# Differential attention: weights left unscaled by the first map's sum, and the norm by heads merged with the output product

## The reference

```
def mix(p):                                # p: softmax of both maps of a head
    p = p.reshape(b, h2 // 2, 2, nq, nk)
    return p[:, :, 0] - lam * p[:, :, 1]
o = attend(q, k, v, mix)
o = rms_norm(o, subln) * (1.0 - lam_init)  # over the 128 columns of each head, EPS = 1e-6
return o.reshape(B, S, DA_HEADS * DA_V_DIM) @ wo
```

## Time and profile before

| | |
|---|---|
| median of 3 runs | 4159.78 us (4154.15 to 4170.31) |
| the profiled execution | 4156.24 us, span 4154.4 us |
| TensorE, VectorE, ScalarE busy | 92%, 78%, 42% of the span |
| mean granted TensorE clock | 0.970 |

### The profile page before, as it was taken

One profiled execution on the slowest core, in us unless ns is written; L12 is line 12 of the kernel. 1 busy time (PEld: TensorE's weight loads), 2 busy tenths in 40 slices (PEclk: granted clock), 3 DMA queues, 4 the chain that ended last, 5 costly groups with the idle time before them and its releaser, 6 DMA issues. The chain is left out here.

```text
span 4154.4 us, 55430 instructions
## 1 busy us (share of the span) xinstructions
PE 3825.5 (92%) x20565; PEld 3167.5 (76%) x20565; DVE 3236.9 (78%) x6703; ACT 1729.2 (42%) x2866; POOL 986.3 (24%) x788
## 2 busy tenths in 40 slices
PE   4999988987999999999979898888679999999998
PEld 1554678856899999999944656887579999999997
DVE  2563845986999999999932434369979999999997
ACT  1112622256444444444423445322754444444443
POOL 0000000046333333333300000000653333333332
PEclk8999989999999999999989999999899999999999
DMA  4420012069999999999930000120599999999996
GB/s 183 154 98 31 1 61 81 24 211 269 420 415 410 407 405 403 402 406 406 378 117 25 18 35 7 61 81 21 142 336 421 418 405 405 401 405 406 407 405 271
DMA packets 267693, 1033.68 MB, mean 249 GB/s; under 512 B 147009, under 2 KB 150017, under 8 KB 159361
## 3 DMA queue, kind: packets, MB, share of 16 engines
q0 software_dynamic: 76032, 553.68, 33.2%
q1 hardware_dynamic: 191392, 476.46, 30.2%
HBM read 970.69 MB, written 59.39 MB: 248 GB/s over the span
## 5 line engine op out<-in xcount | busy, mean ns | idle before, releaser
L1472 POOL DMA_INDIRECT gbuf<-in_uv,rows x340 | 518.1, 1524 | 877.4 <-DVE hT L1639 807.6
L1264 POOL TENSOR_SCALAR pqT<-iota,selT 128x128 f32<-128x128 f32 x256 | 201.7, 805 | 1514.9 <-ACT selT L1205 1464.7
L1639 DVE SCALAR_TENSOR_TENSOR hT<-gbuf,act,hT 128x1024 f32<-128x1024 f32 x336 | 416.8, 1282 | 6.0
L1624 DVE SCALAR_TENSOR_TENSOR gbuf<-gbuf,ht 128x1024 f32<-128x1024 f32 x340 | 402.0, 1219 | 6.1 <-DMA gbuf<-in_uv,rows 5.9
L1472 POOL DMA_INDIRECT xT<-in_uv,rows x172 | 257.6, 1498 | 469.0 <-DVE hT L1639 394.3
L1486 PE MATMUL ps<-h0h,U0h 128*128 128x384 f32 x1024 | 344.7, 337 | 11.1 <-DVE U0l L1598 11.1
L1486 PE MATMUL ps<-h1h,U1h 128*128 128x384 f32 x1024 | 344.8, 337 | 10.0 <-DVE U1l L1598 10.0
L1486 PE MATMUL ps<-h1h,U1l 128*128 128x384 f32 x1024 | 344.4, 336 | 0.0
L1486 PE MATMUL ps<-h0h,U0l 128*128 128x384 f32 x1024 | 344.3, 336 | 0.0
L1486 PE MATMUL ps<-h1l,U1h 128*128 128x384 f32 x1024 | 344.0, 336 | 0.0
L1486 PE MATMUL ps<-h0l,U0h 128*128 128x384 f32 x1024 | 344.0, 336 | 0.0
(11 more groups left out here) (356 smaller groups left out, 9017.4 us busy)
## 6 DMA issues: line engine op xcount, KB each, us to landing
ring<-in_u SPq DMA_DIRECT2D x128, 1024.0 KB, 12.8
ring<-in_v SPq DMA_DIRECT2D x128, 1024.0 KB, 9.2
ring<-in_wts SPq DMA_DIRECT2D x26, 2048.0 KB, 8.4
gates<-ring SPq DMA_DIRECT2D x32, 1536.0 KB, 7.9
ring<-gates SPq DMA_DIRECT2D x64, 768.0 KB, 16.0
xT<-in_ada_late SPq DMA_DIRECT2D x24, 1024.0 KB, 5.0
abuf<-in_ada_mid POOLq DMA_DIRECT2D x16, 1024.0 KB, 5.1
gbuf<-in_uv,rows POOLq DMA_INDIRECT x340, 10.3
```

The costliest lines, as they stand in the source:

```text
L1264: last = pool.tensor_scalar(one2[:, r % 2, t, :], iota[:], selT[:, 1, t0 + t:t0 + t + 1], selT[:, 2, t0 + t:t0 + t + 1], ALU.is_equal, ALU ...
L1472: pool.indirect_dma_start(out=slots[m % GSLOTS], out_offset=None, in_=inp[f"uv{l}"], in_offset=bass.IndirectOffsetOnAxis(ap=rows[:, c:c + ...
L1624: v.scalar_tensor_tensor(u, u, 1.0, ht[:, m // P, :], ALU.mult, ALU.mult, accum_out=act4[:, n % 2, m % 2:m % 2 + 1]).then_inc(sem(n_ + "do ...
L1639: v.scalar_tensor_tensor(y, x, w, y, ALU.mult, ALU.add).then_inc(sem(n_ + "acc"), 1)
```

## The change

In attention the scale of the first map is left out. Its sum goes into a small tensor `zall` [128 x 5 x 8], and the factor of the second map is multiplied by it. A [128 x 1] operation on VectorE now comes between the reciprocal and the combining, which waits for it.

```
                 def weights(w):
                     v.wait_ge(sem("da_exp"), 2 * w + 2)
-                    v.reciprocal(z[:, 6:8], z[:, 4:6]).then_inc(s, 1)
+                    v.reciprocal(z[:, 7:8], z[:, 5:6]).then_inc(s, 1)
                     v.wait_ge(s, at(w, 5))
-                    v.tensor_tensor(z[:, 8:9], z[:, 7:8], lam[:, 4:5], ALU.mult).then_inc(s, 1)
+                    v.scalar_tensor_tensor(z[:, 8:9], z[:, 7:8], lam[:, 4:5], zall[:, qb, hd:hd + 1], ALU.mult, ALU.mult).then_inc(s, 1)
-                    v.tensor_scalar(p0, p0, z[:, 6:7], None, ALU.mult).then_inc(s, 1)
-                    v.wait_ge(s, at(w, 7))
+                    v.wait_ge(s, at(w, 6))
                     v.scalar_tensor_tensor(p0, p1, z[:, 8:9], p0, ALU.mult, ALU.add).then_inc(s, 1)
...
-                                       ..., accum_out=z[:, 4 + c:5 + c])
+                                       accum_out=z[:, 5:6] if c else zall[:, qb, hd:hd + 1])
```

```
+    def diff_out(ring, oT, zall, j0, nxt, sq, rinv, hi, lo, wh, wl):
+            def _(sp):                      # as in out_product: loads of the next chunks
+            def _(pe):
+                def spread(h):
+                    if h >= 2:
+                        pe.wait_ge(sem("sub_v"), h - 1)
+                    for tb in range(TB):
+                        at = tb * HDA + h
+                        mm = pe.matmul(bank2(4 + 2 * (h % 2))[:, tb * P:(tb + 1) * P], rinv[:, at:at + 1].to_broadcast([P, P]),
+                                       ident, start=True, stop=True)
+                    mm.then_inc(sem("sub_bc"), 1)
+                for h in range(HDA):
+                    pe.wait_ge(sem("sub_sq"), h + 1)
+                    for tb in range(TB):
+                        at = tb * HDA + h
+                        mm = pe.matmul(sums[:, at:at + 1], sq[:, h % 2, tb * P:(tb + 1) * P], ones[:, 0:1], start=True, stop=True)
+                    mm.then_inc(sem("sub_mm"), 1)
+                pe.wait_ge(sem("sub_r"), 3)
+                spread(0)
+                spread(1)
+                for nb in range(DC):
+                    pe.wait_ge(sem(n + "wl"), nb + 1)
...
+                    for c in range(DC):
+                        if nb == 0:
+                            pe.wait_ge(sem(n + "ol"), c + 1)
...                                          (the six matmuls of a chunk, as L626 to L630)
+                        if nb == 0 and c + 2 < HDA:
+                            spread(c + 2)
+                    mm.then_inc(sem(n + "mm"), 1)
+            def _(act):
+                for h in range(HDA):
+                    if h >= 2:
+                        act.wait_ge(sem("sub_mm"), h - 1)
+                    act.activation(sq[:, h % 2, :], oT[:, h, :], ACT.Square).then_inc(sem("sub_sq"), 1)
+                    if h in (1, 3):
+                        round_w(h // 2)
+                act.wait_ge(sem("sub_r"), 2)
+                act.activation(rinv[:], rinv[:], ACT.Sqrt, scale=1.0 / VDA).then_inc(sem("sub_sd"), 1)
+                for h in range(HDA):
+                    act.wait_ge(sem("sub_v"), h + 1)
+                    act.copy(hi[:, h, :], oT[:, h, :]).then_inc(sem(n + "oh"), 1)
+                for nb in range(2, DC):
+                    round_w(nb)
+            def _(v):
+                def scaled(h):
+                    v.wait_ge(sem("sub_bc"), h + 1)
+                    v.scalar_tensor_tensor(oT[:, h, :], oT[:, h, :], gains[:, 2:3], bank2(4 + 2 * (h % 2)),
+                                           ALU.mult, ALU.mult).then_inc(sem("sub_v"), 1)
+                def rest_o(h):
+                    v.wait_ge(sem(n + "oh"), h + 1)
+                    v.tensor_tensor(lo[:, h, :], oT[:, h, :], hi[:, h, :].bitcast(F32), ALU.subtract).then_inc(sem(n + "ol"), 1)
+                v.tensor_tensor(z, z, z, ALU.mult).then_inc(sem("sub_r"), 1)
+                rest_w(0)
+                rest_w(1)
+                v.wait_ge(sem("sub_r"), 1)
+                v.wait_ge(sem("sub_mm"), HDA)
+                v.scalar_tensor_tensor(rinv[:], z, VDA * EPS, sums, ALU.mult, ALU.add).then_inc(sem("sub_r"), 1)
+                v.wait_ge(sem("sub_sd"), 1)
+                v.reciprocal(rinv[:], rinv[:]).then_inc(sem("sub_r"), 1)
+                scaled(0)
+                for h in range(HDA):
+                    if h + 1 < HDA:
+                        scaled(h + 1)
+                    rest_o(h)
...                                          (results into xT, as L666 to L673)
```

More of the change, by code:

```diff
@@ L469, in turns @@
                     blocks = (0, 1, 2, 3, 5) if qb < 4 else (4,)
-                    pe.wait_ge(sem("da_w"), 8 * (w + 1) + (4 if w + 1 < len(items) else 0))
+                    pe.wait_ge(sem("da_w"), 7 * (w + 1) + (4 if w + 1 < len(items) else 0))
                     if w >= 1:
@@ L506, in at @@
                     if k <= 4:
-                        return k if w == 0 else 8 * w - 4 + k
-                    return 8 * w + k + (4 if w + 1 < M else 0)
+                        return k if w == 0 else 7 * w - 3 + k
+                    return 7 * w + k + (4 if w + 1 < M else 0)
                 def maxima(w):
@@ L520, in weights @@
                 def weights(w):
-                    n, z = width(items[w][1]), z_(w)
+                    hd, qb = items[w]
+                    n, z = width(qb), z_(w)
                     v.wait_ge(sem("da_exp"), 2 * w + 2)
-                    v.reciprocal(z[:, 6:8], z[:, 4:6]).then_inc(s, 1)
+                    v.reciprocal(z[:, 7:8], z[:, 5:6]).then_inc(s, 1)
                     v.wait_ge(s, at(w, 5))
-                    v.tensor_tensor(z[:, 8:9], z[:, 7:8], lam[:, 4:5], ALU.mult).then_inc(s, 1)
+                    v.scalar_tensor_tensor(z[:, 8:9], z[:, 7:8], lam[:, 4:5], zall[:, qb, hd:hd + 1], ALU.mult, ALU.mult).then_inc(s, 1)
                     p0, p1 = pr[:, w % 3, 0, 0:n], pr[:, w % 3, 1, 0:n]
-                    v.tensor_scalar(p0, p0, z[:, 6:7], None, ALU.mult).then_inc(s, 1)
-                    v.wait_ge(s, at(w, 7))
+                    v.wait_ge(s, at(w, 6))
                     v.scalar_tensor_tensor(p0, p1, z[:, 8:9], p0, ALU.mult, ALU.add).then_inc(s, 1)
@@ L545, in exps @@
                     for c in range(2):
-                        act.wait_ge(sem("da_w"), 2 * c + 2 if w == 0 else 8 * w - 2 + 2 * c)
+                        act.wait_ge(sem("da_w"), 2 * c + 2 if w == 0 else 7 * w - 1 + 2 * c)
                         act.activation(pr[:, w % 3, c, 0:n], bank2(2 * c, n), ACT.Exp, bias=z[:, 2 + c:3 + c],
-                                       scale=rsq[:, 2, qb, 2 * hd + c:2 * hd + c + 1], accum_out=z[:, 4 + c:5 + c]).then_inc(sem("da_exp"), 1)
+                                       scale=rsq[:, 2, qb, 2 * hd + c:2 * hd + c + 1],
+                                       accum_out=z[:, 5:6] if c else zall[:, qb, hd:hd + 1]).then_inc(sem("da_exp"), 1)
                 def copies(w):
@@ L569, in _ @@
                         results(w - 3)
-    def diff_subnorm(indT, oT, scr):
+    def diff_out(ring, oT, zall, j0, nxt, sq, rinv, hi, lo, wh, wl):
+        n = "wo_"
+        sums = ps[:, 2, 0:TB * HDA]
+        parts = ((0, 0, 320), (0, 320, TS), (1, TS, T))
         with nc.Block() as block:
+            @block.sync
+            def _(sp):
+                read = {j0 + c: (sem(n + "wl"), 4 * (c + 1)) for c in range(2)}
+                for j in nxt:
+                    load_chunk(sp, ring, j, read)
+            @block.tensor
+            def _(pe):
[18 more added lines that the diff above has]
+                    pe.wait_ge(sem(n + "wl"), nb + 1)
+                    if nb >= 4:
+                        pe.wait_ge(sem(n + "v"), 3 * (nb - 3))
+                    for c in range(DC):
+                        if nb == 0:
+                            pe.wait_ge(sem(n + "ol"), c + 1)
+                        for w, o in ((wh, hi), (wl, hi), (wh, lo)):
+                            for half in range(2):
+                                mm = pe.matmul(ps[:, 2 * (nb % 4) + half, 0:320], w[:, nb % 2, c, :],
+                                               o[:, c, 320 * half:320 * (half + 1)], start=c == 0 and w is wh and o is hi,
+                                               stop=c == DC - 1 and o is lo)
+                        if nb == 0 and c + 2 < HDA:
+                            spread(c + 2)
+                    mm.then_inc(sem(n + "mm"), 1)
@@ L574, in _, with round_w @@
             @block.scalar
             def _(act):
+                def round_w(nb):
+                    j = j0 + nb // 4
+                    if nb % 4 == 0:
+                        chunk_in(act, j)
+                    if nb >= 2:
+                        act.wait_ge(sem(n + "mm"), nb - 1)
+                    w = ring[:, j % SLOTS, :].rearrange("p (c n) -> p c n", c=DC)
+                    act.copy(wh[:, nb % 2], w[:, :, (nb % 4) * P:(nb % 4 + 1) * P]).then_inc(sem(n + "wh"), 1)
                 for h in range(HDA):
@@ L578, in _ @@
```

(30 more changed lines are left out.)

7 lines of the change are left out of this document (2 added, 5 removed).

## The result

The changed kernel takes 4172.23 us (median of 22 runs, 4163.75 to 4177.71), the kernel before 4167.8 us (22 runs, 4154.15 to 4172.59) beside it. The ratio is 1.0015, interval 1.0008 to 1.0022: 6 us slower, 3 to 9. That is inside the range and within 0.5% as forecast, on the side that was forecast; the 2.0 us of the forecast lie a little under the interval. The forecast time, 4161.8 us, is 10.4 us under the measured median; 8.0 of these are the kernel before itself, whose first three runs had a median of 4159.78 us and whose 22 have 4167.8.

A forecast was written before the change was run, and what follows sets the result against it. TensorE was busy 92% of the span; the score-bank loop was taken to pace attention. Attention -0.6 and first block +2.6 gave +2.0 us on the 4159.78 median: 4161.8 us, range 4148 to 4178.

The forecast's parts named there:

- Attention, -0.6: Attention stage: the loop through the score banks sets the pace, so dropping the scale gains only 0.6 us, bounds 0 and 16.
- the two full distances a head: Attention: two maximum-to-maximum distances per head, each expected to shrink from 3.62 to 3.58 us, 0.04 us gained each.
- Sums: Head sums after attention: one-column matmuls let the clock fall some 4 us in, so they end at 547.4 us.
- Rival 1: Head sums: the clock stays up through them; 5.0 us faster in all, 4154.8 us; chance 27%.
- Root: After the head sums: addition, root, reciprocal and hand-overs take 1.2 us, in place of 5.4.
- First two spreads: After the root: two dense spreads at half clock take 4.8 us and bring the clock back.
- Rounds: First output block, head by head: six serial rounds of 4.0 us, TensorE waiting on the remainder, at full clock.
- rival 2: First output block: half clock throughout, pauses in the rounds deciding it; 14.6 us slower, 4174.4 us; chance 15%, whole or part.
- Sum: Whole kernel: attention -0.6, first block +2.6, seven later blocks 0, together +2.0 us.
- the last products: End of the first output block, behind the sixth round: products of the last head, 1.0 us.

## Why the prediction was right, and where it was off

**Attention, -0.6.** Measured: -0.3, in the profiled execution and in the comparison behind the first head. The mechanism stands: two runs that took more or less from VectorE show the loop's 3.58 us as the floor and VectorE's own time as the limit only above it. Of the two full distances a head only one came down to 3.58; the other stayed 3.62 (406.12 to 409.74) with VectorE idle 0.32 us, so it had not been VectorE's.

**Sums.** Said: the clock falls 4 us in, end 15.0 us after attention's. Measured: it fell 3 us in, end 15.8 us after. In all five profiles with one-column sums it fell in them (14.4 to 16.2 us for the eight heads), and in none of the four with 128 columns were they longer than 12 us. From start to start a record is 0.112 us at full clock, less than the 0.12 that the prediction read from rows 8 with the tail in it, and 0.213 us at half. At full clock 80 would take 9.0 us, so the clock cost 5.8 us of the 14.72. Rival 1 is excluded in these five profiles. By the rule on weight loads in the Trainium skill, "TensorE: Matmul & The Clock Gate", section on LDWEIGHTS, the eight heads would be an estimated 8.5 us; the 9.0 us at full clock are near it, the 14.72 measured are not.

**Root.** 1.2 us said, 1.1 measured (547.35 to 548.42). **First two spreads.** 4.8 said, 4.4 measured, nearly all at half clock. With weights that repeat one column a record takes 0.112 us at full clock and 0.213 at half, as in the sums.

**Rounds: the step that did not hold.** The prediction said of the pauses in each round: "attention's tail had gaps too and the clock held, so I expect it to hold." At full clock the round is 3.97 us as worked out (4.0), and the wait is the one named. But the clock fell at 555.9 and stayed low for two rounds: 4.72 and 5.51 us for the first two (554.65, 559.37, 564.88). That is 2.3 us more than six rounds of 3.97, and most of the 2.7 us between the 48.6 us forecast for the end and the 51.3 measured. Of the three profiles with one-column sums and rounds of this kind it held in one (48.8 us) and fell in two (51.3, 53.6); with wide sums and these rounds it held in the one profile there is (41.9). So the likeliest case was a mixture of the forecast and rival 2, to which (or to a part of which) I had given 15%, and the size was off by that. Why the clock falls in one execution and holds in another stays open.

**Sum.** +2.0 said; +4.9 by stages, +6 (3 to 9) in the runs. The 1.7 us in the norm behind are the clock again, for which the prediction has no term. That the time came out right is in part the width of the range: 4148 to 4178 holds the median of every kernel run here, also that of the one that is 16 us faster (4149.73). The account by stages is the better check: attention, root and first spreads are within 0.4 us of what was said, the sums end 0.8 us later, the rounds are 2.1 us longer than six of 4.0, and the last products 0.3 us.

## What to carry to other kernels

An operation taken from an engine is worth only its excess over the next loop: find the loop (here score bank, maximum, exponential, 3.58 us) at a place where the engine had little to do, and compare. When stages are merged item by item, write the round out once per engine, in program order, and ask for each instruction what stands in front of it: two lines moved ahead of a wait halved the round, and with the wider sums turned 6 us of loss into 16 us of gain. A matmul of one column isn't cheap: here it took as long as one of 128, and during a long train of them the clock fell and stayed low, which cost 5.8 us. Where one column is needed, streaming all 128 cost nothing and kept or regained the clock in four profiles of four.

## What the runs showed of the hardware

One moving column and 128 take the same time in f32 with 128 weight columns: 0.112 us from start to start at full clock and 0.213 us at half, in either form. With the narrow form the granted clock went from 2.4 to 1.2 GHz in five profiles of five and stayed there to the end of the sums, although TensorE's busy column and its weight loads had no gap (11.65 and 11.56 of 11.7 us). With 128 columns it fell in one of four, and rose again while the sums ran. The clock also fell in rounds where full-width work alternated with pauses of 1.8 us, in two profiles of four.
